# A ring of 20 units in pieces of 4 MB for the expert weights of a decoder block

## What is computed

```
h   = rms_norm(x);  proj = h @ w_in                      # retention + pooling mixers, gates
x   = x + merged(proj) @ w_out
h2  = rms_norm(x);  logits = h2 @ w_router + b_router    # 32 experts, top 4, softmax
for e in 32 experts:                                     # on the tokens routed to e
    gu  = h2[tokens of e] @ w_gate_up[e] + b_gate_up[e]  # 1024 -> 2 x 1024
    act = (clip(up) + 1) * min(gate, 7) * sigmoid(1.702 * min(gate, 7))
    x  += weight * (act @ w_down[e] + b_down[e])         # 1024 -> 1024
h3  = rms_norm(x)
x   = x + sigmoid(h3 @ w_ple_gate) * (p @ w_ple_proj)    # the per-layer embedding
y   = rms_norm(x)
```

## Time and profile before

| | |
|---|---|
| median of three runs | 1264.03 us (1262.73 to 1264.06) |
| the profiled execution's own time | 1262.35 us |
| its span, first to last instruction | 1260.5 us |
| busy: TensorE, VectorE, ScalarE | 1156.8, 391.9, 201.3 us |
| mean granted clock of TensorE | 0.977 |
| SyncE's queue (q1) | 451.98 MB, 86.9% of 16 engines' span |
| read from HBM | 455.28 MB, 362 GB/s over the span |
| chain that ended last | PE 57%, DMA 39%, DVE 2% |

### The profile page before, as it was taken

One profiled execution on the slowest core, in us unless ns is written; L12 is line 12 of the kernel. 1 busy time (PEld: TensorE's weight loads), 2 busy tenths in 40 slices (PEclk: granted clock), 3 DMA queues, 4 the chain that ended last, 5 costly groups with the idle time before them and its releaser, 6 DMA issues.

```text
span 1260.5 us, 13315 instructions
## 1 busy us (share of the span) xinstructions
PE 1156.8 (92%) x5340; PEld 599.4 (48%) x5341; DVE 391.9 (31%) x620; ACT 201.3 (16%) x267; POOL 8.0 (1%) x19
## 2 busy tenths in 40 slices
PE   7999999989998989889999998998989998989787
PEld 5888888863343433333333433342433433333236
DVE  6964755631030312212221212130303122121126
ACT  5354444320000000000000000000000000000024
POOL 0000000000000000000000000000000000000000
PEclk9999999999899999999999999999998999999999
DMA  9855455769699999999899999999999999999970
GB/s 344 296 169 164 137 196 194 284 258 384 274 428 427 427 430 427 429 427 428 363 428 429 428 428 428 427 428 427 428 427 428 391 429 429 427 429 427 428 311 34
DMA packets 56089, 456.98 MB, mean 363 GB/s; under 512 B 5342, under 2 KB 6796, under 8 KB 30252
## 3 DMA queue, kind: packets, MB, share of 16 engines
q1 hardware_dynamic: 53740, 451.98, 86.9%
q10 hardware_dynamic: 2304, 4.37, 1.0%
HBM read 455.28 MB, written 1.05 MB: 362 GB/s over the span
## 4 chain that ended last, share of the span: by engine, by line
PE 57%; DMA 39%; DVE 2%; issue 1%; SPq 1%; ACT 0%; DVEq 0%; POOLq 0%; POOL 0%; ACTq 0%
PE ps L563 55%; DMA ring<-in_w_down 21%; DMA ring<-in_w_gate_up 18%; PE ps L570 1%; PE ps L829 1%; SPq L477 0%; SPq L472 0%; DMA x<-in_x 0%; PE ps L845 0%; DVE B L1481 0%; DVE over_xn L1272 0%; ACT B L1148 0%; DVE B L1494 0%; DVE x L1409 0%; DVE B L1490 0%
## 5 line engine op out<-in xcount | busy, mean ns | idle before, releaser
L563 PE MATMUL ps<-ring,B 128*64 128x512 f32 x3040 | 685.4, 607 | 71.7 <-DMA ring<-in_w_gate_up 47.6
L563 PEld LDWEIGHTS ps<-ring,B 128*64 128x64 f32 x3040 | 233.2, 140 | 509.8 <-issue 507.1
L1485 DVE TENSOR_SCALAR B<-ps 128x1024 f32<-128x1024 f32 x16 | 19.6, 1225 | 462.5 <-PE ps L563 462.5
L563 PE MATMUL ps<-w_split,over_hT 128*128 128x512 f32 x480 | 153.4, 396 | 2.7 <-DVE w_split L1264 2.7
L1264 DVE TENSOR_TENSOR w_split<-ring,w_split 128x1024 fp32r<-128x1024 f32 x80 | 96.3, 1224 | 68.6 <-ACT w_split L1022 68.3
L1139 ACT ACTIVATE B<-B 128x1024 f32<-128x1024 f32 x16 | 16.9, 1057 | 598.7 <-DVE B L1485 598.7
L563 PEld LDWEIGHTS ps<-w_split,over_hT 128*128 128x128 f32 x480 | 90.9, 191 | 21.7 <-issue 3.1
L563 PE MATMUL ps<-w_split,over_xn 128*128 128x512 f32 x256 | 100.7, 393 | 0.0
L1022 ACT CAST w_split<-ring 128x1024 fp32r<-128x1024 f32 x80 | 83.2, 1055 | 103.2 <-PE ps L563 103.2
L563 PE MATMUL ps<-B 128*128 128x512 f32 (+3 forms) x280 | 90.3, 497 | 2.2 <-ACT B L1148 1.2
L563 PEld LDWEIGHTS ps<-B,xn 128*128 128x128 f32 x512 | 62.8, 200 | 13.3 <-issue 13.3
(11 more groups left out here) (151 smaller groups left out, 462.8 us busy)
## 6 DMA issues: line engine op xcount, KB each, us to landing
ring<-in_w_gate_up SPq DMA_DIRECT2D x120, 2048.0 KB, 17.1
ring<-in_w_down SPq DMA_DIRECT2D x64, 2048.0 KB, 17.1
ring<-in_w_in SPq DMA_DIRECT2D x28, 1024.0 KB, 5.2
ring<-in_w_gate_up SPq DMA_DIRECT2D x12, 1024.0 KB, 9.4
ring<-in_w_branch SPq DMA_DIRECT2D x8, 1024.0 KB, 6.9
ring<-in_w_out SPq DMA_DIRECT2D x4, 1024.0 KB, 5.1
B<-in_w_gate_up SPq DMA_DIRECT2D x4, 1024.0 KB, 6.3
ring<-in_w_ple_gate SPq DMA_DIRECT2D x4, 1024.0 KB, 16.4
```

Of the source, the lines that this page charges most:

```text
L563: return pe.matmul(out, lhsT, rhs, start=start, stop=stop, skip_group_check=True)
L1485: step(ve.tensor_scalar(gate, two_banks(0), LIMIT, None, ALU.min), s.gate_ready)
```

## The change

All experts' weights after the first pair's gate_up come in pieces of 4 MB: 32 KB a partition, four rows of w_gate_up or all eight rows of w_down, consecutive in memory. A turn has 4 pieces of w_gate_up and 2 of w_down. The ring has 20 units, five places of four units. The buffers B2 to B8 and hT of the mixer are now its units 12 to 19, and the routing's small buffers lie over the mixer's constants. The 16 fine pieces of the first pair lie in units 0 to 15; place 4 (units 16 to 19) is filled once the router's matmuls are done. A class works out beforehand which place each piece takes and at what count of `used` it is free; from piece 70 on (in turn 12) place 4 is retired and takes w_proj and p, which SyncE's queue now loads, and the last two pieces are kept off place 1.

The sigmoid is written over the gate, so it starts behind the product (up + 1) * gate instead of beside it, and ScalarE waits for the second product before it copies the output of down over `up`. TensorE's transposes of the product take columns with a stride of 8 instead of 4, and the gather columns with a stride of 4 instead of 2. All turns are written out; the loops are gone. The turns with extra work are 11 (route), 12 (output bias) and 13 (embedding) instead of 8, 11 and 5.

```diff
-SLOTS, SLOT = 12, 2048
+SLOTS, SLOT = 20, 2048
-BIG = 2 * SLOT
+UNITS = 4
+UP_ROWS, DOWN_ROWS = UNITS, 2 * UNITS
+UPS, DOWNS = 2 * KD // UNITS, KD // UNITS
+PER_TURN = UPS + DOWNS
+PLACES = SLOTS // UNITS
 FINE = 2 * KD
-BIG_UP, PER_TURN = KD, KD + KD // 2
-RING = (0, 1, 2, 4, 5, 3)
-BIGS = len(RING)
-FINE_RING = (0, 1, 2, 3, 4, 5, 8, 9, 10, 11, 6, 7)
-EMBED_TURN, ROUTE_TURN, BIAS_TURN = 5, 8, 11
+MIXER_BUFFERS = (8, 7, 2, 4, 6, 3, 5, "hT")
+FINE_UNITS = (12, 13, 14, 15, 0, 1, 2, 3, 8, 9, 10, 11, 4, 5, 6, 7)
+LATE_PLACES = (8, 9) if UNITS == 2 else (4,)
+BIGS = (PAIRS - 1) * PER_TURN + DOWNS
+ROUTE_TURN, BIAS_TURN, EMBED_TURN = 11, 12, 13
+LAST_DOWN = (0, 1, 2, 3, 12, 13, 14, 15)
...
+class Ring:
+    def __init__(self):
+        free = [(0, at) for at in LATE_PLACES]
+        free += [(f + UNITS, FINE_UNITS[f] // UNITS) for f in range(0, FINE, UNITS)]
+        self.place, self.free_at, self.nth = [], [], []
+        had = [0] * PLACES
+        self.retired = None
+        for g in range(BIGS):
+            if self.retired is None and g >= (EMBED_TURN - 2) * PER_TURN and free[0][1] == PLACES - 1:
+                self.retired = (g, free.pop(0)[0])
+            last = g >= BIGS - DOWNS
+            taken = next(i for i, (_, at) in enumerate(free) if not last or UNITS * at in LAST_DOWN)
+            value, at = free.pop(taken)
+            had[at] += 1
+            self.place.append(at)
+            self.free_at.append(value)
+            self.nth.append(had[at])
+            if not last:
+                free.append((FINE + g + 1, at))
...
+            def load_up(at, m, e):
+                w = t["w_gate_up"][0, bass.ds(e, 1), UP_ROWS * P * m:UP_ROWS * P * (m + 1), :]
+                sp.dma_start(place(at), w.rearrange("e (p j) n -> p (e j n)", j=UP_ROWS)).then_inc(loaded[at], 16)
...
+            def load_big(pair, q, down):
+                g = chunk_number(pair, q, down)
+                if g >= len(LATE_PLACES):
+                    sp.wait_ge(used, RING.free_at[g])
...
+            def load_embedding():
+                sp.wait_ge(used, RING.retired[1])
+                sp.dma_start(w_proj, t["w_ple_proj"][0].rearrange("(c p) n -> p c n", p=P)).then_inc(proj_loaded, 16)
+                sp.dma_start(p_in, t["p"][0, 0].rearrange("(i p) n -> p i n", p=P)).then_inc(p_loaded, 16)
...
+            sp.wait_ge(logitT_psum, 1)
+            for q in range(len(LATE_PLACES) - 1, UPS):
+                load_big(1, q, False)
+            for q in range(DOWNS):
+                load_big(0, q, True)
+            for turn in range(2, PAIRS):
+                for q in range(UPS):
+                    if chunk_number(turn, q, False) == RING.retired[0]:
+                        load_embedding()
+                    load_big(turn, q, False)
...
             def act_to_width(s, pair):
                 for half in range(2):
-                    pe.wait_ge(s.act_ready, 2 * pair + half + 1)
+                    pe.wait_ge(s.act_ready, 2 * pair + (half + 1 if DOWN_ROWS == 4 else 2))
...
             def down(s, pair, bank=4):
                 for c in range(KD):
                     if c % 4 == 0:
                         pe.wait_ge(s.actT_ready, 2 * pair + 1 + c // 4)
-                        for h in range(2):
-                            down_ready(pe, s, pair, h, c)
-                    both(s, pair, down_weights, actT, c, D, bank, c % 4 == 3)
+                    for h in range(2):
+                        down_ready(pe, s, pair, h, c)
+                    both(s, pair, down_weights, actT, c, D, bank, c % DOWN_ROWS == DOWN_ROWS - 1)
...
-            with pe.Fori(2, EMBED_TURN) as turn:
-                pair_turn(turn)
...
+            for turn in range(2, PAIRS):
+                pair_turn(turn, is_last=turn == PAIRS - 1)
+                if turn == ROUTE_TURN:
+                    route_rest(turn)
+                if turn == BIAS_TURN:
+                    output_bias(turn)
+                if turn == EMBED_TURN:
+                    project_ple(turn)
...
             def sigmoid(s, pair):
                 e.wait_ge(s.gate_ready, pair + 1)
-                nc.scalar.activation(sig, gate, ACT.Sigmoid, scale=ALPHA).then_inc(s.sig_ready, 1)
+                nc.scalar.activation(gate, gate, ACT.Sigmoid, scale=ALPHA).then_inc(s.sig_ready, 1)
...
                 sigmoid(first, turn)
+                e.wait_ge(first.act_ready, 2 * turn + 2)
                 read_down(first, turn - 1)
...
-                step(ve.tensor_scalar(gate, two_banks(0), LIMIT, None, ALU.min), s.gate_ready)
+                step(ve.tensor_scalar(gate, two_banks(0), LIMIT, None, ALU.min))
...
-                step(ve.scalar_tensor_tensor(up, up, 1.0, gate, ALU.add, ALU.mult))
+                step(ve.scalar_tensor_tensor(up, up, 1.0, gate, ALU.add, ALU.mult), s.gate_ready)
...
             def read_ple():
                 for i in range(4):
-                    dve.wait_ge(ple_psum, i + 1)
+                    if i % 2 == 0:
+                        dve.wait_ge(ple_psum, i + 2)
```

More of the change, by code:

```diff
@@ L241, in build @@
         count_top_f = piece(1)[0:1, :]
-        w_router = router[:, 0:KD * N_EXPERTS].rearrange("p (k e) -> p k e", k=KD)
-        b_router = router[:, KD * N_EXPERTS:]
+        w_router = piece(KD * N_EXPERTS).rearrange("p (k e) -> p k e", k=KD)
+        b_router = piece(N_EXPERTS)
         logitT = piece(SEQ)[0:N_EXPERTS, :]
[L245 to L249, removed]
+        scatterT = piece(SEQ)
+        onehot = piece(SEQ).rearrange("p (t s) -> p t s", t=TILES)
+        weighted = piece(SEQ).rearrange("p (t s) -> p t s", t=TILES)
+        pT = piece(2 * SEQ).rearrange("p (c s) -> p c s", c=2)
+        assert at[0] <= N_CONST - DMAT
+        p_in = ring[:, P_UNIT, 0:TILES * SEQ].rearrange("p (t n) -> p t n", t=TILES)
+        w_proj = ring[:, PROJ_UNIT, :].rearrange("p (c n) -> p c n", c=2)
+        ple = rows(ring[:, PROJ_UNIT, :])
+        b_down = late[0:N_EXPERTS, 0:D]
+        g_final = late[:, D:2 * D]
+        tail_scratch = ring[:, LAST_DOWN[4], 0:D]
         result = rows(B[0])
@@ L292, in build @@
         more = ExpertSemaphores(sem, "more")
-        used, loaded = first.chunk_used, first.loaded
-        fine_loaded = mixer_loaded + [sem(f"fine_loaded{i}") for i in range(MIXER_SLOTS, SLOTS)]
+        used = first.chunk_used
+        loaded = [sem(f"loaded{i}") for i in range(PLACES)]
+        fine_loaded = mixer_loaded + [sem(f"fine_loaded{i}") for i in range(MIXER_SLOTS, FINE)]
+        gate_loaded = [sem(f"gate_loaded{i}") for i in range(len(PLE_RAW))]
         block = ctx.enter_context(nc.Block())
@@ L332, in big_slot, with chunk_number @@
[L332 to L337, removed]
+            return s is first and pair == 0
+        def chunk_number(pair, q, down):
+            turn = pair + 1 if down else pair
+            if turn == PAIRS:
+                return (PAIRS - 1) * PER_TURN + q
+            return (turn - 1) * PER_TURN + (UPS if down else 0) + q
@@ L339, in up_weights, with place_of, place @@
+        def place_of(s, pair, q, down):
+            if s is first:
+                return RING.place[chunk_number(pair, q, down)]
+            return ((UPS if down else 0) + q) % MORE_PLACES
+        def place(at):
+            return ring[:, UNITS * at:UNITS * (at + 1), :].rearrange("p a n -> p (a n)")
         def up_weights(s, pair, h, c):
             if is_fine(s, pair):
-                return fine_slot(2 * c + h)
-            return big_slot(2 * (c // 2) + h)[:, (c % 2) * SLOT:(c % 2 + 1) * SLOT]
+                return ring[:, FINE_UNITS[2 * c + h], :]
+            at = place_of(s, pair, 2 * (c // UP_ROWS) + h, False)
+            return place(at)[:, (c % UP_ROWS) * SLOT:(c % UP_ROWS + 1) * SLOT]
@@ L355, in used_down @@
+            return FINE + (chunk_number(pair, UPS, False) if pair else 0)
         def used_down(s, pair):
@@ L474, in load_down @@
[L474 to L482, removed]
-                else:
-                    load_down(first, q, (q - BIG_UP) // 2, 2 * turn - 2 + q % 2)
-            def load_early(f):
-                former = MIXER_CHUNKS - 1 - (MIXER_CHUNKS - 1 - f) % MIXER_SLOTS
+                m = c // UP_ROWS
@@ L521, in _ @@
-            with sp.Fori(2, PAIRS) as turn:
-                for q in range(PER_TURN):
-                    sp.wait_ge(used, PER_TURN * turn + q + FINE - PER_TURN - BIGS + 1)
-                    load_turn(q, turn)
-            for q in range(KD // 2):
-                sp.wait_ge(used, PER_TURN * (PAIRS - 1) + q + FINE - BIGS + 1)
-                load_down(first, q, q // 2, N_EXPERTS - 2 + q % 2)
+            for unit in (8, 9, 10, 11, 6, 7):
+                load_after_piece(unit)
+            sp.wait_ge(logitT_psum, 1)
@@ new lines, in _ @@
+            for q in range(len(LATE_PLACES) - 1, UPS):
[7 more added lines that the diff above has]
+                    load_big(turn, q, False)
+                for q in range(DOWNS):
```

(11 more changed lines are left out.)

258 lines of the change are left out of this document (107 added, 151 removed).

## The result

The changed kernel takes 1267.7 us, the median of twelve runs (1264.82 to 1271.44), beside 1264.05 for the kernel before (1262.73 to 1265.48): a ratio of 1.0031, 95% interval 1.0024 to 1.0039. It is 3.7 us slower; 5.1 were forecast. The profiled execution took 1267.13 us, its span 1265.3, beside 1262.35 and 1260.5.

What follows compares the result with a forecast made beforehand. The prediction took the experts' stage to be bound by the transfer of its 402.7 MB of weights. Terms -12.0 - 3.5 + 3.2 + 8.2 + 9.2 = +5.1 on the 1264.03 us median gave 1269.1, range 1256 to 1279.

Steps and rivals of the forecast that it cites:

- the head start: Step 1, at the start: full-rate stream from 337.8 with five pieces done, against 330.2 with three; -12.0 us.
- the packet: Step 2, in the weight stream: 32 KB packets instead of 16 KB give 0.4% on 87 pieces; -3.5 us.
- Step 6: Effects priced at nothing: longer activation chain, transposes with stride 8, gather with stride 4 inside 6 us of room, unrolled loops.
- Loads: Step 3, turn 12: w_proj and p move into the stream ahead of piece 70; +3.2 us.
- Late turns: Step 4, turns 12 and 13: bias and embedding idle DMA 5.6 and 10.0 us with four places, against 2.7 and 4.7; +8.2.
- The cover: In step 4, extra TensorE work that four places absorb before DMA idles: 2.5 us.
- the 2 us for an emptied ring: In step 4, a ring that runs empty costs 2 us over the schedule, added for the bias; its counterpart at the embedding likewise.
- End: Step 5, last down: both experts' w_down must land whole, so 16.4 us behind the last landing against 7.2; +9.2.
- (a): Late turns absorb their extra work, the cover of four places being 10 us: 1256, half of it 1262.6; chance 0.17.
- (b): Every piece of the stream: the packet pays 1.4%, 1260.6 us; kernels level at 432.8 GB/s; chance 0.13.
- (c): A wash: an empty ring costs nothing beyond the schedule (-4), the end 1 us less; 1264 us; chance 0.21.
- (d): A slower stream, 0.8% and more in each piece, +10 on the forecast, 1279 us; chance 0.09.

Runs made afterwards that it cites:

- e1: Changed kernel with ScalarE writing the normed tokens so that the gather reads its stationary operand without a stride: 1268.5 us, ratio 1.0043 to the kernel before.
- e9: Changed kernel with only piece 0 (place 4) waiting until TensorE has used up two fine units: 1267.7 us, ratio 1.0034 to the kernel before.
- e5: Changed kernel with each 4 MB piece coming as two loads of 16 KB a partition, places and order kept: 1275.1 us, ratio 1.0087 to the kernel before.
- e3: Changed kernel without the embedding's work and its loads, place 4 never retired, so five places to the end: 1250.9 us, ratio 0.9899 to the kernel before.
- e10: Changed kernel without the embedding's work (loads and retired place stay), route at turn 7 and output bias at turn 9: 1259.4 us.
- e2: Changed kernel without the embedding's work, its two loads and the retired place kept: 1264.5 us, ratio 1.0001 to the kernel before.
- e4: Changed kernel with the route at turn 7 instead of 11 and the output bias at turn 9 instead of 12: 1266.3 us.
- e6: Changed kernel with the last down's two pieces in halves of 2 MB, TensorE waiting for a half at a time: 1267.35 us.
- e7: Changed kernel with the w_down pieces of the last two pairs in halves of 2 MB: 1262.6 us, ratio 0.9988 to the kernel before.
- e8: Changed kernel with UNITS = 2, so pieces of 2 MB in ten places, nine after the retired one: 1244.9 us, ratio 0.9859 to the kernel before.

## Why the prediction was right, and where it was not

The end of the last down moved from 1219.8 to 1211.47 + 13.94 = 1225.4, +5.6 in the profiled executions for +5.1 forecast. 39.9 us follow it instead of 40.7, so these two executions are 4.8 apart; the medians are 3.7 apart. The forecast was right in its mechanisms, and its sum was lucky in part: the head start was 3.2 too large and the packet 2.5 too small, and these two misses nearly cancel. By steps:

1. **Head start, -12.0; measured -8.8.** The stream is at its full rate from 341.0 with five pieces done, against 330.2 with three: 10.8 - 2 x 9.80. The term was mis-sized at gate_up(1), which began 4.0 later than before and not 1.1. Step 6 put the stride of 4 "inside the 6 us of room", but gather(0) and gather(1) have no room, since they are on the path to gate_up(1). By e1 they are 2.2 us of it, up to 3.6 without the lower clock of e1's first gather; the chain through the sigmoid took 1.2 where I had 1.1. (The 319.5 of step 1 took the bias at full clock; gate_up(1) began at 320.3.) e9 shows that the release by gate_up(1) sets the step.
2. **Packet, -3.5; about -6.** 431 against 428 GB/s, 0.07 us on each of 87 pieces (the rates are rounded to whole GB/s, which leaves about 2 us either way). That is 0.7%, between the 0.4% by half of the step from 8 to 16 KB and the 1.4% by the packets of 2 KB, nearer to the first. e5 shows it with 7.4 in the medians, the size of the load halved too.
The Trainium skill ("DMA: Bandwidth & Descriptors", Where 436 GB/s comes from) gives 435.2 as the ceiling; 431 is beneath it, so the trace agrees.
The same page of the Trainium skill (Latency and other measured facts) has copies at 207 GB/s with a row pitch of 512 KiB and at 103 with 4 MiB, where its full rate was 214. No run here has such a pitch; 32 KB lost nothing against 16, 431 against 428.
3. **Loads, +3.2; about +3.1 by the stream's rate.** Not measured alone; they are a part of the 8.5 us between e3 and e10.
4. **Late turns, +8.2; measured about +9.** Against 431 GB/s the windows lack 2.4 and 3.4 us in 1020 to 1060 and 8.5 in 1100 to 1120; forecast were 5.6 and 10.0, each where it was said. From 341.0 to the last landing at about 1210.0 are 869 us, of which 87 pieces take 846.6 and the loads 3.1: 19.3 are left. Before, from 330.2 to 1212.6, 178 pieces of 4.90 leave 10.2. That is +9.1, of which the windows with dips hold 14.3 - 7.4 = 6.9. The sum is near, its inner prices are not: e2, e4 and e10 show that the bias and the embedding don't add up (5.1 and 6.9 alone, 8.3 together), and beside e3 they leave some 5 for the four places themselves. The cover had the gather in its loop, where e1 shows that it isn't. In the working on the ring before, 597.0 and six pieces of 4.90 are 626.4 and not 625.8, so the idle time by the schedule is 2.0 and the windows show 2.7 beyond it. No run tests the 2 us for an emptied ring alone.
5. **End, +9.2; about +8.2.** From the landing at 1190.54 it is 34.9 to the end of down (35.9 forecast); with 19.5 us for the last pair that is 15.4 behind the last landing, against 7.2. The steps between the last two downs took 5.1 and not 6.0. e6 and e7 show that the last landing no longer bounds the end.
6. **At nothing.** True for the unrolled loops and the longer activation in ordinary turns, where the stream kept 431 GB/s; wrong for the gather at the start. In the late turns e1 shows the gather's 3.7 us to be free, for a reason that I didn't give: DMA's 19.5 us stand beside it.

Together: -8.8 - 6.0 + 3.1 + 9.1 + 8.2 = 5.6. Step 4 is counted as what the other terms leave, so this sum can't test it; its dips alone do.

Of the rivals, (a) is refused by the windows (the dips sum to 14 us and more), (b) by 431 where it needed 432.8. (c), the wash, would have had the dips without the 2 us each that an emptied ring costs; the result is 1.1 us above its edge, and the interval excludes no change. It is refused by its number alone. (d) needed a slower stream, and the stream is faster.

## What to carry to other kernels

With a ring of fixed bytes, the size of a piece buys rate in tenths of a percent (0.7% from 16 to 32 KB a partition) and pays in grain: what is freed as a whole (9 us at the start alone, between e8 and the changed kernel), what must have landed as a whole, and what one retired place takes away. Here 2 MB pieces in ten places beat 4 MB in five by 22.8 us. Price a ring by the longest time that passes between two releases against the bytes that are free or queued by then, and in the last turns follow the consumer and not the stream. A saving counts only where it stands in the loop that sets the pace: 3.7 us in each of 16 gathers bought nothing that the medians show.

## What the runs showed of the hardware

- A weight load of 128x128 floats took 192 ns with contiguous columns (e1), 197 with a stride of 2 and 329 with a stride of 4 floats. I had taken the stride to be free up to 1 us a turn.
- One load of 32 KB a partition and packet runs at 431 GB/s, two of 16 KB into the same place at 428, with a DMA share of 1.00 to 1.01 in both.
- TensorE after a wait of 4.57 us took 15.47 us for the down that takes 13.95 after one of 0.71. The length of the wait alone doesn't set it: in e1 a down took 13.96 after 3.53 us, in the changed kernel one took 15.65 after 2.60. Work taken from TensorE in a turn that DMA bounds comes back as a wait, and the granted clock beside it is lower (0.979 over the changed kernel, 0.963 over e1).
